# A gating layer's first projection as seven products instead of eight, and where GpSimd issues the sums of its weights

## The chip, the cores and the metric

The kernel runs on one core of a Trainium2 chip. The metric is the time of one execution in microseconds (us) on the device: 1015.75 us as the median of three runs of the kernel before (1014.75 to 1017.11). A run counts once; lower is better. Engines are called TensorE (PE in the rows), VectorE (DVE), ScalarE (ACT), GpSimd (POOL) and SyncE (SP). SP and POOL issue most of the transfers.

## The reference, cut to what matters

Four sublayers work on 512 tokens of 1024 channels, each followed by a residual sum and a layer norm. The one that the change rewrites is the second mixer:

```python
def chunked_spatial_gating(x, w_in, b_in, ln_g, ln_b, w_s, b_s, w_out, b_out):
    z = jax.nn.gelu(x @ w_in + b_in, approximate=False)
    u, v = jnp.split(z, 2, axis=-1)
    v = layer_norm(v, ln_g, ln_b)
    ...
    s = jnp.einsum("gts,bnsgc->bntgc", w_causal, v) + b_s.T[:, :, None]
    return (u * s) @ w_out + b_out

def reference(x, ...):
    for i in range(DEPTH):                       # DEPTH = 2
        y = conformer_conv_module(x, ...) if i == 0 else chunked_spatial_gating(x, ...)
        x = layer_norm(DEEPNORM_ALPHA * x + y, norm1_g[i], norm1_b[i])
        y = conv_ffn(x, ...)
        x = layer_norm(DEEPNORM_ALPHA * x + y, norm2_g[i], norm2_b[i])
    return x
```

`w_in` is 1024 x 2048. Its second half makes `v` (called GV below), its first half makes `u` (GU). All arithmetic is float32.

## The kernel before, in words

**Stages.** In order of time: the convolution's input projection with its 31 taps (to about 132 us), its output projection (to about 182), the first feed-forward (up to about 420, down to 531), gating (to about 670) and the second feed-forward (to the end).

**Weights.** All weights lie in DRAM as units of 128 x 1024 values (512 KB). A unit passes four steps: SP loads it into one of four `raw` slots (L532), ScalarE rounds it to its high part `wh` (`his`, L767), VectorE makes the low part `wl = raw - wh` (`los`, L1280), and TensorE uses it in three matmuls per tile: high x high, high x low, low x high. `w_used` counts the units that TensorE is done with, `w_lo` those whose low part is there. SP loads unit u only when the low part of unit u - 4 is made; ScalarE and VectorE write into the ring slot of unit u only when unit u - 4 of the ring is used. In the convolution some units have their low part made by an accumulating transfer that GpSimd issues (`lo`, L613).

**Strassen already in place.** The feed-forward's down projection takes seven products of half-size blocks instead of eight. Sums of its weight blocks are made in DRAM (`summed`): SP copies pieces of the units (`copies`, L538 to L540) and GpSimd issues accumulating transfers of 128 x 512 values on top (L702) and copies of that size (L704), one after the other as `w_used` advances (`summed_weights`).

**Gating before.** TensorE computes GV from eight units: the first four by token block (`down_by_block`), with the last transposes of the norm before in between, then four by channel (`down_by_k`); 192 matmuls of 512 columns. VectorE adds the bias row out of PSUM (L1943), ScalarE applies Gelu, VectorE takes statistics (L1948), and adds the scaled residual for later (`residual`, L1548, four instructions). After the last statistics VectorE aggregates them (L1958), GpSimd takes the roots of the four token blocks (`mixer_root`, L593 and L588), and VectorE normalizes block after block: L1962, L1966 (waits for the root), `los` of GU unit 4 + t, and the low part of v (L1970). Meanwhile TensorE computes the eight GU units of 24 matmuls each, waiting for each unit's low part; after the seventh it begins the spatial products (L2400), which need all four blocks of v.

**Orders are fixed by hand.** Each engine has one list of instructions, written out in the order of the code, and takes them strictly one after the other. A wait holds all that stands behind it on that engine, the issue of transfers on SP and GpSimd included. On GpSimd the convolution's part is, in this order: the adds of tap products for the last channel group, first token half (`add_last(0, ...)`), three adds for the second half, one `lo` transfer, four more adds, and the root of the first half (`mixer_root(0, 1, 0, HT)`), for which VectorE waits before it can centre the first token half (L1428).

The lines on which the prediction leans most, from the kernel before:

```python
        add_last(0, 1, LAST_GP[0])
        add_last(1, 1, 4)
        lo(BY_DMA[-1])
        add_last(1, 4, ROOT_AT)
        mixer_root(0, 1, 0, HT)
...
        for t in range(NT):
            mixer_root(ROOTS + 2 * NT + t, ROOTS + t + 1, t, 1)
```

## Time and profile before

| What | Value |
|---|---|
| median of 3 runs | 1015.75 us (1014.75 to 1017.11) |
| the profiled execution, its own time | 1015.58 us |
| its span (first to last instruction) | 1013.8 us |
| granted TensorE clock, share of full | 0.998 |
| TensorE matmuls, busy share of the span | 99% |
| VectorE | 86% |
| ScalarE | 60% |
| GpSimd | 23% |
| traffic of HBM over the span | 229 GB/s |

The profiled execution lies 0.17 us under the median, and 1.8 us of its time lie outside the span. The busy shares are averages over stages that differ; a matmul's record overlaps the next one's, so that the pace is read from distances between starts.

### The profile page before, as it was taken

Reading aid. Unit: us, or ns where it says so; the run is one execution under the profiler, and the core shown is the slowest. Engines: PE = TensorE matmul, PEld = TensorE weight load, DVE = VectorE, ACT = ScalarE, POOL = GpSimd, SP = SyncE. Lnnn points to the kernel's source line nnn. Section 1 sums busy time; section 2 is a strip of 40 time slices with the busy share of each in tenths; the row PEclk is TensorE's granted clock in tenths of the full one; section 3 lists DMA queues with packets and bytes.
Section 4 is the critical chain, followed back from the end, with each engine's and each line's share of the span. In section 5 each row is a group of like instructions: output and inputs, shape, how many; then the busy total and the mean of one; then the engine's idle time right before and its main releaser. Section 6 shows DMA issues by size and latency. Waiting matters only on the chain.

```text
span 1013.8 us, 15746 instructions
## 1 busy us (share of the span) xinstructions
PE 1003.6 (99%) x5379; PEld 861.1 (85%) x5379; DVE 867.6 (86%) x1228; ACT 604.5 (60%) x903; POOL 233.3 (23%) x289
## 2 busy tenths in 40 slices
PE   9999999999999999999999999999999999999997
PEld 7777788988899988888888888898988999888885
DVE  6999977897988988898894878779888888879888
ACT  7889865564565556666454343457555555566653
POOL 2998730023232121000010210002423212100001
PEclk9999999999999999999999999999999999999999
DMA  9766269369889676376555333825989966627652
GB/s 342 218 161 166 58 147 349 119 196 238 236 211 228 220 169 173 102 271 208 195 179 194 118 111 107 307 79 186 262 237 229 220 209 173 163 98 260 205 197 112
DMA packets 65590, 194.02 MB, mean 191 GB/s; under 512 B 7552, under 2 KB 8576, under 8 KB 65024
## 3 DMA queue, kind: packets, MB, share of 16 engines
q1 hardware_dynamic: 44144, 137.76, 39.1%
q0 software_dynamic: 19376, 48.24, 23.7%
q10 hardware_dynamic: 2016, 7.34, 2.1%
q8 instruction: 28, 0.46, 0.2%
q14 instruction: 26, 0.21, 0.1%
HBM read 178.11 MB, written 54.53 MB: 229 GB/s over the span
## 4 chain that ended last, share of the span: by engine, by line
PE 78%; DVE 5%; DMA 3%; issue 2%; ACT 1%; SPq 0%; DVEq 0%; POOL 0%; POOLq 0%; ACTq 0%
PE ps L2017 10%; PE ps L2018 10%; PE ps L2019 10%; PE ps L2306 6%; PE ps L2307 6%; PE ps L2308 6%; PE ps L2259 5%; PE ps L2260 5%; PE ps L2261 5%; PE ps L2027 4%; PE ps L2028 4%; PE ps L2029 4%; DMA raw<-d_weights 3%; PE ps L2186 1%; DVE ps L1618 1%
## 5 line engine op out<-in xcount | busy, mean ns | idle before, releaser
L2017 PE MATMUL ps<-xh,wh 128*128 128x512 f32 x528 | 208.5, 395 | 0.3 <-DVE wl L1280 0.3
L2018 PE MATMUL ps<-xl,wh 128*128 128x512 f32 x528 | 205.7, 390 | 0.0
L2019 PE MATMUL ps<-xh,wl 128*128 128x512 f32 x528 | 205.6, 389 | 0.0
L767 ACT ACTIVATE wh<-raw 128x1024 fp32r<-128x1024 f32 x114 | 119.9, 1057 | 80.4 <-PE ps L2308 49.5
L1280 DVE TENSOR_TENSOR wl<-raw,wh 128x1024 fp32r<-128x1024 f32 x101 | 123.2, 1224 | 32.9 <-ACT wh L767 32.5
L702 POOL DMA_DIRECT2D summed<-d_weights x88 | 75.2, 1115 | 198.0 <-PE ps L2019 96.4
L2017 PEld LDWEIGHTS ps<-xh,wh 128*128 128x128 f32 x528 | 99.2, 188 | 22.0 <-issue 1.2
L2019 PEld LDWEIGHTS ps<-xh,wl 128*128 128x128 f32 x528 | 99.1, 188 | 21.0
L2018 PEld LDWEIGHTS ps<-xl,wh 128*128 128x128 f32 x528 | 99.2, 188 | 20.7 <-issue 1.2
L2306 PE MATMUL ps<-wh,parts 128*128 128x512 f32 x264 | 102.9, 390 | 0.0
L2308 PE MATMUL ps<-wh,parts 128*128 128x512 f32 x264 | 102.7, 389 | 0.0
L2307 PE MATMUL ps<-wl,parts 128*128 128x512 f32 x264 | 102.7, 389 | 0.0
L1607 DVE TENSOR_TENSOR wl<-raw,wh 128x1024 fp32r<-128x1024 f32 x62 | 75.6, 1220 | 22.5 <-ACT wh L1014 22.5
L599 POOL TENSOR_SCALAR veps<-sqs 128x1 f32<-128x1 f32 x15 | 4.8, 323 | 385.2 <-ACT squares_down L961 266.2
L1376 DVE SCALAR_TENSOR_TENSOR ps<-glu,par,ps 128x512 f32<-128x512 f32 x125 | 84.7, 752 | 0.6 <-PE ps L2103 0.4
L622 POOL TENSOR_TENSOR gsum<-gsum,prods 128x512 f32<-128x512 f32 x53 | 70.2, 1324 | 14.5 <-ACT prods L836 8.4
L1014 ACT ACTIVATE wh<-raw 128x1024 fp32r<-128x1024 f32 x62 | 65.6, 1058 | 8.2 <-DMA raw<-d_weights 8.2
L1618 DVE SCALAR_TENSOR_TENSOR ps<-vpad,par,ps 128x512 f32<-128x512 f32 x80 | 60.3, 753 | 8.0 <-ACT ps L1038 2.2
L1618 DVE SCALAR_TENSOR_TENSOR ps<-gpad,par,ps 128x512 f32<-128x512 f32 x80 | 60.2, 753 | 6.4 <-DVE ps L1618 2.1
L2306 PEld LDWEIGHTS ps<-wh,parts 128*128 128x128 f32 x264 | 49.5, 188 | 11.1 <-DVE wl L1280 0.8
L2308 PEld LDWEIGHTS ps<-wh,parts 128*128 128x128 f32 x264 | 49.5, 188 | 10.4
L2307 PEld LDWEIGHTS ps<-wl,parts 128*128 128x128 f32 x264 | 49.6, 188 | 10.2
(266 smaller groups left out, 2543.9 us busy)
## 6 DMA issues: line engine op xcount, KB each, us to landing
raw<-d_weights SPq DMA_DIRECT2D x156, 512.0 KB, 4.9
raw<-summed SPq DMA_DIRECT2D x56, 512.0 KB, 4.1
summed<-d_weights POOLq DMA_DIRECT2D x88, 256.0 KB, 9.5
summed<-d_weights SPq DMA_DIRECT2D x66, 256.0 KB, 5.2
summed<-summed POOLq DMA_DIRECT2D x46, 256.0 KB, 4.8
res<-brow POOLq DMA_DIRECT2D x12, 512.0 KB, 10.7
wl<-raw POOLq DMA_DIRECT2D x4, 1024.0 KB, 6.9
wl<-raw POOLq DMA_DIRECT2D x5, 512.0 KB, 6.3
```

The costliest lines, as they stand in the source:

```text
L702: eng.dma_start(out, of, accum_op=ALU.add).then_inc(w_sum[i % AHEAD], 16)
L767: eng.activation(split_at(u)[0], raw[:, u % RAW, :], ACT.Copy).then_inc(w_hi, 1)
L1280: eng.tensor_tensor(l, raw[:, u % RAW, :], h.bitcast(f32), ALU.subtract).then_inc(w_lo, 1)
L1376: eng.scalar_tensor_tensor(out=ps[:, bank, :], in0=glu[:, j % 2, k:k + SEQ], scalar=par[:, c:c + 1], in1=ps[:, bank, :], op0=ALU.mult, op1 ...
L1607: eng.tensor_tensor(wl[:, slot, :], raw[:, part, :], wh[:, slot, :].bitcast(f32), ALU.subtract).then_inc(w_lo, 1)
L1618: eng.scalar_tensor_tensor(out=accs[v], in0=buf[:, off:off + SEQ], scalar=par[:, bass.ds(cw, 1)], in1=accs[v], op0=ALU.mult, op1=ALU.add). ...
L2017: eng.matmul(ps[:, bank, cols], a, xh[:, k, cols], start=(k == 0), stop=False)
L2018: eng.matmul(ps[:, bank, cols], a, xl[:, k, cols], start=False, stop=False)
L2019: mm = eng.matmul(ps[:, bank, cols], b, xh[:, k, cols], start=False, stop=(k == KD - 1))
L2306: eng.matmul(ps[:, bank + t, :], s_h, w_h[:, cols], start=first, stop=False)
L2307: eng.matmul(ps[:, bank + t, :], s_h, w_l[:, cols], start=False, stop=False)
L2308: mm = eng.matmul(ps[:, bank + t, :], s_l, w_h[:, cols], start=False, stop=last)
```

## The change

GV is computed by Strassen's scheme in Winograd's form: seven products of 256 tokens x 512 channels x 512 columns, 168 matmuls instead of 192. For that

- the weights of GV come as four units as before in another layout, two units of a fourth-product sum, four units with the sums for the fifth and sixth product, and four with those for the third and seventh: six units more than before, ten of them from a new DRAM tensor `gsum`. The first GU unit stands between the products as `U_GU0`;
- the sums in `gsum` are made by twelve SP copies of 128 x 512, issued behind the loads of the convolution's first four output units (`gv_copies`), by two accumulating transfers of 512 x 512 that GpSimd issues in the convolution, between the adds of the two token halves, and by ten more transfers that it issues behind the feed-forward's sums (`up_sums(0)`);
- sums of token blocks are made, rounded and split by VectorE and ScalarE (`gn5`, `gs2`, `gs4`, `gv7`), after copies of three blocks (`a11f`, `a12f`, `a22f`) by ScalarE;
- VectorE puts the products together in `vtm` (`gv_rd` counts);
- the residual's bias row of gating is added by four accumulating transfers that GpSimd issues, each behind a wait for one more used unit, and the scaling moves into the later sum (`half_sum`); the four VectorE instructions of `residual` are gone;
- some rows of parameters are loaded elsewhere in ScalarE's list.

The core of the diff (`...` where it is cut):

```diff
@@ build_trunk, SyncE
+        def gv_copies(i):
+            w1, w2 = weights_d[raw_gv + i], weights_d[raw_gv + GQ + i]
+            eng.dma_start(gsum_d[2 + i, :, 0:HALF], w1[:, 0:HALF]).then_inc(gv_copied, 16)
+            eng.dma_start(gsum_d[2 + GQ + i, :, HALF:UNIT], w2[:, 0:HALF]).then_inc(gv_copied, 16)
+            eng.dma_start(gsum_d[2 + GQ + i, :, 0:HALF], w2[:, HALF:UNIT]).then_inc(gv_copied, 16)
...
+            if u == U_GV + GQ:
+                eng.wait_ge(gv_sum, 16 * (4 + 2 * GQ))
             load(u % RAW, u)
+            if 0 <= u - U_CONV_OUT < GQ:
+                gv_copies(u - U_CONV_OUT)
@@ GpSimd, convolution
         add_last(0, 1, LAST_GP[0])
+        eng.wait_ge(gv_copied, 16 * 3 * GQ)
+        eng.dma_start(fifth[:, :, first], w2[:, :, first], accum_op=ALU.add).then_inc(gv_sum, 16)
+        eng.dma_start(third[:, :, second], w2[:, :, second], accum_op=ALU.add).then_inc(gv_sum, 16)
         add_last(1, 1, 4)
@@ GpSimd, behind the feed-forward's sums
         up_sums(0)
+        eng.wait_ge(gv_sum, 16 * 2)
+        eng.dma_start(fifth[:, :, second], fifth[:, :, first]).then_inc(gv_sum, 16)
+        eng.wait_ge(gv_sum, 16 * 3)
+        eng.dma_start(fifth[:, :, second], w2[:, :, second], accum_op=ALU.add).then_inc(gv_sum, 16)
...
@@ GpSimd, gating
         eng.affine_select(out=wsraw[:, :, :], ...
+        eng.wait_ge(br3_ok, 1)
+        eng.wait_ge(x_ok, 2 * NT)
+        eng.wait_ge(xt, 2 * 2 * NT)
+        for t in range(NT):
+            eng.wait_ge(w_used, U_GU + 1 + t)
+            eng.dma_start(res[:, t, :], brow[:, :], accum_op=ALU.add).then_inc(res3_add, 16)
         for t in range(NT):
             mixer_root(ROOTS + 2 * NT + t, ROOTS + t + 1, t, 1)
@@ VectorE, gating (the four residual instructions gone, among others these new)
-                residual(2)
+            eng.tensor_tensor(gn5[:, :, cols], ps[:, B0[1] + 2 * t, :].rearrange("p (k n) -> p k n", k=4), a22f[:, :, cols],
+                              ALU.subtract).then_inc(ga_sum, 1)
+            eng.tensor_tensor(gs2[:, :, cols], gn5[:, :, cols], a11f[:, :, cols], ALU.subtract).then_inc(ga_sum, 1)
...
+        eng.wait_ge(w_used, U_GU + 1)
+        for t in halves:
+            eng.wait_ge(gv_rd, G_C12 - 1 + t)
+            eng.tensor_tensor(vtm[:, 2 + t, c2], ps[:, 4 + t, :], vtm[:, 2 + t, c2], ALU.subtract).then_inc(gv_rd, 1)
@@ TensorE, gating
-        down_by_block(U_GV, 4, 4, xh, xl, 0, KD, last_block, lambda t: wait_x(1, t))
-        down_by_k(U_GV + 4, 4, 0, xh, xl, 0, KD)
+        def gv(u, c, bank, tokens, i, t):
...
+        for t in range(NT // 2):
+            wait_x(1, t)
+            for i in range(GQ):
+                if t == 0:
+                    eng.wait_ge(*lo_of(U_GV + i))
+                mm = gv(U_GV + i, 0, 4, g11, i, t)
...
+        eng.wait_ge(*lo_of(U_GU0))
+        eng.wait_ge(gv_rd, G_C11)
+        up(split_at(U_GU0), GU_BANK[0]).then_inc(w_used, 1)
...
+        for i in range(GQ):
+            gv_third(i)
+            if i == 0:
+                eng.wait_ge(gv_rd, G_MP4)
+            if i < GQ - 2:
+                gv_seventh(i)
+        gv_seventh(GQ - 2)
+        gv_seventh(GQ - 1)
...
-        for j in range(KD):
+        for j in range(1, KD):
             eng.wait_ge(*lo_of(U_GU + j))
```

How the lists of instructions move, at three places. First GpSimd in the convolution, from the adds of the first token half of the last channel group to the first root. Before (L631 are the adds, L613 the `lo` transfer, L593 and L588 the root):

```order
L622 TENSOR_TENSOR gsum<-gsum,prods 128x512 [waits gp_add,gp_prod] x5
L631 TENSOR_TENSOR gsum<-gsum,prods 128x256 [waits gp_add,gp_prod] x11
L613 DMA wl<-raw 128x1024 [waits w_neg]
L631 TENSOR_TENSOR gsum<-gsum,prods 128x256 [waits gp_add,gp_prod] x4
L593 TENSOR_SCALAR veps<-mv 128x2 [waits var_ok]
L588 TENSOR_TENSOR rstd<-veps,half_m 128x2 [waits eps_ok]
```

And now the same stretch of GpSimd, where L682 are the adds, L724 and L725 the new transfers and L644 and L639 the root:

```order
L673 TENSOR_TENSOR gsum<-gsum,prods 128x512 [waits gp_add,gp_prod] x5
L682 TENSOR_TENSOR gsum<-gsum,prods 128x256 [waits gp_add,gp_prod] x8
L724 DMA gsum<-d_weights 512x512 [waits gv_copied]
L725 DMA gsum<-d_weights 512x512
L682 TENSOR_TENSOR gsum<-gsum,prods 128x256 [waits gp_add,gp_prod] x3
L664 DMA wl<-raw 128x1024 [waits w_neg]
L682 TENSOR_TENSOR gsum<-gsum,prods 128x256 [waits gp_add,gp_prod] x4
L644 TENSOR_SCALAR veps<-mv 128x2 [waits var_ok]
L639 TENSOR_TENSOR rstd<-veps,half_m 128x2 [waits eps_ok]
```

Two transfers of 512 rows each have come to stand ahead of seven adds, one transfer and the root.

Second, GpSimd in gating, from the mask of the spatial weights to the roots of the four token blocks. Before (L743 is the mask, L593 and L588 the root of one block):

```order
L743 AFFINE_SELECT wsraw<-wsraw 128x1024 [waits gm_in]
L593 TENSOR_SCALAR veps<-mv 128x1 [waits var_ok]
L588 TENSOR_TENSOR rstd<-veps,half_m 128x1 [waits eps_ok]
L593 TENSOR_SCALAR veps<-mv 128x1 [waits var_ok]
L588 TENSOR_TENSOR rstd<-veps,half_m 128x1 [waits eps_ok]
```

And now on the same engine, with L815 as the transfers of the residual's row:

```order
L808 AFFINE_SELECT wsraw<-wsraw 128x1024 [waits gm_in]
L815 DMA res<-brow 128x1024 [waits xt,w_used,x_ok,br3_ok]
L815 DMA res<-brow 128x1024 [waits w_used] x3
L644 TENSOR_SCALAR veps<-mv 128x1 [waits var_ok]
L639 TENSOR_TENSOR rstd<-veps,half_m 128x1 [waits eps_ok]
```

Four transfers, each behind a wait for TensorE, have come to stand ahead of the roots.

Third, VectorE in gating behind those roots, as it is now (L2139 aggregates, L2143 and L2147 normalize block 0, L1395 is the low part of GU unit 4, L2151 that of v):

```order
L2139 BN_AGGR mv<-stats 128x2 [waits st_ok]
L2139 BN_AGGR mv<-stats 128x2 x3
L2143 SCALAR_TENSOR_TENSOR vtm<-vtm,mv,glg 128x1024 [waits var_ok,gm_in]
L2147 SCALAR_TENSOR_TENSOR vtm<-vtm,rstd,glb 128x1024 [waits rstd_ok,st_ok]
L1395 TENSOR_TENSOR wl<-raw,wh 128x1024 [waits w_hi,w_used]
L2151 TENSOR_TENSOR vl<-vtm,vh 128x1024 [waits v_hi]
```

This stretch stands as it stood before the change; only the line numbers differ.

## Rows read from the trace of the kernel before

**Rows 1.** The page: span; busy us (share of the span) xinstructions of each engine.

```profile
span 1013.8 us, 15746 instructions
PE 1003.6 (99%) x5379; PEld 861.1 (85%) x5379; DVE 867.6 (86%) x1228; ACT 604.5 (60%) x903; POOL 233.3 (23%) x289
```

**Rows 2.** Waits of TensorE, 400 to 1000 us: who for whom, us, times, longest.

```profile
PE ps L2351 <- DVE wl L1280: 0.2, 1, 0.2
```

**Rows 3.** Timeline of TensorE: start, us, line, xcount; start of GU and of spatial(0).

```profile
570.64 0.39 PE L2017 MATMUL ps<-xh,wh 128*128 128x512 f32 x1
...
608.72 0.28 PE L2400 MATMUL ps<-wsp,vh 128*128 128x256 f32 x1
```

**Rows 4.** Two stretches: length; PE, PEld, DVE, ACT, POOL busy; clock, DMA.

```profile
105.00:130.00 25.00, 24.89 (x149) 19.90 (x147) 24.59 (x47) 20.02 (x40) 19.61 (x23) 1.00 0.30 71
...
524.00:571.00 47.00, 47.00 (x220) 38.95 (x219) 31.17 (x38) 16.21 (x22) 4.16 (x5) 1.00 0.56 188
```

**Rows 5.** Timeline of GpSimd: residual row by transfers; the first root in gating.

```profile
284.66 3.59 POOL L687 DMA_DIRECT2D res<-brow  x4 [1.84 <-PE ps L2261]
...
577.86 0.24 POOL L593 TENSOR_SCALAR veps<-mv 128x1 f32<-128x1 f32 x1 [16.62 <-DVE mv L1958]
```

**Rows 6.** Timeline of VectorE in gating: residual, low parts, GV, behind the roots.

```profile
560.19 5.53 DVE L1548 SCALAR_TENSOR_TENSOR res<-res,brow 128x1024 f32<-128x1024 f32 x4
565.64 2.35 DVE L1280 TENSOR_TENSOR wl<-raw,wh 128x1024 fp32r<-128x1024 f32 x2
570.84 1.29 DVE L1943 TENSOR_TENSOR vtm<-ps,gvrow 128x512 f32<-128x512 f32 x2 [2.85 <-PE ps L2029]
...
579.70 1.29 DVE L1966 SCALAR_TENSOR_TENSOR vtm<-vtm,rstd,glb 128x1024 f32<-128x1024 f32 x1 [0.53 <-POOL rstd L588]
580.90 1.22 DVE L1280 TENSOR_TENSOR wl<-raw,wh 128x1024 fp32r<-128x1024 f32 x1
...
586.91 1.22 DVE L1280 TENSOR_TENSOR wl<-raw,wh 128x1024 fp32r<-128x1024 f32 x1
...
597.86 1.23 DVE L1970 TENSOR_TENSOR vl<-vtm,vh 128x1024 fp32r<-128x1024 f32 x1
```

**Rows 7.** Timeline of GpSimd, end of the convolution.

```profile
113.27 9.76 POOL L631 TENSOR_TENSOR gsum<-gsum,prods 128x256 f32<-128x256 f32 x11
123.46 0.87 POOL L613 DMA_DIRECT2D wl<-raw  x1 [0.43 <-ACT wl L769]
...
127.84 0.26 POOL L593 TENSOR_SCALAR veps<-mv 128x2 f32<-128x2 f32 x1
128.18 0.73 POOL L588 TENSOR_TENSOR rstd<-veps,half_m 128x2 f32<-128x2 f32 x1
```

**Rows 8.** Timeline, VectorE and TensorE, at the first centred block.

```profile
129.02 1.12 DVE L1428 TENSOR_SCALAR ctm<-ctm,mv,rstd 128x128 f32<-128x128 f32 x4
...
129.70 0.28 PE L2131 MATMUL ps<-gluh,diagl 128*128 128x256 f32 x1
129.82 0.38 PE L2170 MATMUL ps<-ident,ctm 128*128 128x128 f32 x2
```

**Rows 9.** Timeline of GpSimd: accumulating and plain transfers of 128 x 512.

```profile
228.12 1.65 POOL L702 DMA_DIRECT2D summed<-d_weights  x2 [3.47 <-PE ps L2261]
...
266.47 1.56 POOL L704 DMA_DIRECT2D summed<-summed  x3 [2.00 <-DMA summed<-d_weights]
```

**Rows 10.** L613, low parts by transfer: waits for it (us, times); time to landing.

```profile
  PEld ps L2017: 0.3, 1
...
DMA to landing us min/median/max: 4.4/6.8/8.6
```

**Rows 11.** Timeline of SP: loads in the convolution.

```profile
96.91 0.80 SPq L532 DMA_DIRECT2D raw<-d_weights  x2
```

**Rows 12.** SP's copies (L539), issue in ns and time to landing.

```profile
L539 SPq DMA_DIRECT2D summed<-d_weights x22: 587/598/1389, 152.3 to 702.2; - x22
...
DMA to landing us min/median/max: 3.9/5.2/10.5
```

More of the change, by code:

```diff
@@ L679, in _ @@
             eng.dma_start(res[:, t, :], brow[:, :], accum_op=ALU.add).then_inc(res0_ok, 16)
-        first, second = slice(0, HALF), slice(HALF, UNIT)
         issued = [0] * AHEAD
@@ L1150, in ffn_down @@
                     rows()
+                if layer == 0 and i == 2 * KQ + 5:
+                    eng.wait_ge(q_add, 6)
+                    row(gvrow[:, :], R_GVB, gv_in)
                 if i == KQ:
@@ L1542, in norm @@
                 block_lo(n, NT - 1)
-        def residual(n):
-            eng.wait_ge(bo_in, 16 * n)
-            for t in range(NT):
-                eng.scalar_tensor_tensor(out=res[:, t, :], in0=res[:, t, :], scalar=ALPHA, in1=brow[:, :],
-                                         op0=ALU.mult, op1=ALU.add).then_inc(res_ok, 1)
         def low_row(layer, q):
@@ new lines, in _ @@
+        los([U_G56 + 2])
+        eng.tensor_tensor(both_rows[:, :], gvrow[:, c1], gvrow[:, c2], ALU.add).then_inc(rows_ok, 1)
+        los([U_G56 + 3])
+        for t in halves:
+            token_lo(gs4l, gs4, gs4h, t, 4 + 2 * t + 1)
+            token_lo(gv7l, gv7, gv7h, t, 4 + 2 * t + 2)
+        los([U_G37])
+        eng.wait_ge(w_used, U_GU0)
+        eng.wait_ge(rows_ok, 1)
+        for t in halves:
+            eng.tensor_tensor(vtm[:, 2 + t, c2], vtm[:, 2 + t, c1], both_rows[:, :], ALU.subtract).then_inc(n_ok, 1)
@@ new lines, in _ @@
+        eng.wait_ge(gv_rd, G_M)
+        for t in range(NT // 2):
+            wait_x(1, 2 + t)
+            for i in range(GQ):
+                u = U_GV + GQ + i // 2
+                if t == 0 and i % 2 == 0:
+                    eng.wait_ge(*lo_of(u))
+                mm = gv(u, i % 2, 4, g22, i, t)
+                if t == 1 and i % 2:
+                    mm.then_inc(w_used, 1)
+        eng.wait_ge(*lo_of(U_GU0))
+        eng.wait_ge(gv_rd, G_C11)
+        up(split_at(U_GU0), GU_BANK[0]).then_inc(w_used, 1)
@@ new lines, in _, with gv_third @@
+        for i, t in ((0, 0), (1, 0), (0, 1), (1, 1), (2, 0), (2, 1), (3, 0), (3, 1)):
+            u = U_G56 + i
+            eng.wait_ge(ga_lo, 2 * t + 2)
+            if t == 0:
+                eng.wait_ge(*lo_of(u))
+            gv(u, 0, 0, gn5p, i, t)
+            mm = gv(u, 1, 2, gs2p, i, t)
+            if t == 1:
+                mm.then_inc(w_used, 1)
+        def gv_third(i):
+            eng.wait_ge(*lo_of(U_G37 + i))
+            for t in range(NT // 2):
+                mm = gv(U_G37 + i, 0, 6, gs4p, i, t)
+            if i == GQ - 1:
+                mm.then_inc(gv_pe, 1)
```

285 lines of the change are left out of this document (218 added, 67 removed).

## Prediction

> **What bounds the kernel now.** I read the page first: TensorE is busy for 99% of a span of 1013.8 us, VectorE for 86%, GpSimd for 23% [rows 1]. The waits of TensorE say how to take this: from 400 to 1000 us, which holds all of gating, it waits 0.2 us in all [rows 2]. So a matmul that is gone is time gained as long as no one else becomes late, and a new wait of TensorE is paid in full. The timeline gives the pace: from the start of GU to the start of spatial(0) lie seven units of 24 matmuls, 168 in 608.72 − 570.64 = 38.08 us, which is 0.2267 us a matmul or 5.44 us a unit [rows 3]. Then I looked for places where another engine stands just ahead of TensorE. In the convolution's last 25 us VectorE is busy for 24.59 and GpSimd for 19.61 [rows 4]; in GV's stretch VectorE has 31.17 of 47 us and GpSimd 4.16 [rows 4]. The sum is made against the profiled execution's 1015.58 us (1013.8 and 1.78 outside the span); the median of the runs is 0.17 us higher, which I let go.
>
> **1. The product itself: −5.44.** 192 matmuls become 168, all of the same shape: 24 x 0.2267 = 5.44 us. GU's first unit only changes its place.
>
> **2. GpSimd's four residual transfers in gating: +5.67.** Call E the end of GV's products, the first GU unit among them; that is 570.64 + 5.44 = 576.1 in terms of before's GV and GU0, but what counts are distances from E. The new L815 transfers wait for `w_used`, the first for E, the second to fourth for the ends of GU units 1, 2 and 3. Behind them on GpSimd stand the four roots; behind the first root on VectorE stand block 0's scaling (L2147) and then the low part of GU unit 4, which TensorE needs right after unit 3. This is a closed chain: TensorE finishes unit 3, and only then does work begin that unit 4 needs.
> Its length: wake GpSimd 0.11 (the gap between the root's end, 128.18 + 0.73, and VectorE's start at 129.02 [rows 7, 8]); issue of the fourth transfer 0.90 (3.59 / 4 [rows 5]); root to VectorE's start 579.70 − 577.86 = 1.84 [rows 5, 6]; scaling 580.90 − 579.70 = 1.20 and low part 1.22 [rows 6]; wake TensorE 0.11. The sum is 5.38. The convolution's root took 128.18 + 0.73 − 127.84 = 1.07, and 0.11 to wake VectorE [rows 7]: with it 4.7. I take 5.0. Before, this low part was ready at 582.12 and wanted at 570.64 + 4 x 5.44 = 592.4, so there were 10 us to spare, and the change uses all of them.
> From there VectorE needs 586.91 − 580.90 = 6.01 us to the next low part, where TensorE needs 5.44: +0.57. Spatial(0) stands behind unit 6 and waits for the last `vl`, which ends 597.86 + 1.23 − 580.90 = 18.19 after the first low part's start; TensorE is there 1.33 + 3 x 5.44 + 0.57 = 18.23 after it [rows 6]: +0.1 at most, for the wake. The residual's transfers themselves are wanted only by the later sums and cost nothing more.
>
> **3. VectorE in GV's stretch: +0.5.** It loses the four `residual` instructions, 5.53 us, and gets six more low parts at 2.35 / 2 = 1.18, which is 7.1, and by my count of the lists some 29 more instructions over 128 x 512 at 1.29 / 2 = 0.65, which is 18.7 [rows 6]. 31.17 − 5.53 + 7.1 + 18.7 = 51.4 of 47 us [rows 4]: VectorE is full, and part of its work runs over E. There the units' low parts 1 to 3 have already been made or have 5 us each, so that the surplus is mostly hidden, by the very wait of step 2 too. Inside GV the product sums stand one bank ahead of TensorE. Bounds: 0, and 1.8, which is one low part and one 512-column step late. I take 0.5.
>
> **4. Two transfers of 512 rows in the convolution: +4.07.** They stand behind 8 of the 11 adds, at 113.27 + 8 x 0.887 = 120.4, and ahead of three adds, the `lo` transfer, four adds and the root [rows 7]. VectorE starts L1428 0.11 us after the root, and TensorE takes the centred block at 129.82 with its last other matmul started at 129.70 [rows 8]: there is about 0.1 to spare. GpSimd's only idle time on the way is 0.43 ahead of L613 [rows 7]. So with x as the cost of one issue the path loses 2x − 0.53.
> No row shows an issue of 512 rows. From below, x is no less than that of an accumulating transfer of 128 rows, 1.65 / 2 = 0.82 [rows 9]; from above it is four times that, 3.3. A part of the 0.82 can't grow with the rows: L613 moves rows of 1024 elements for 0.87 [rows 7], so size is not what counts, and an accumulating issue costs 0.82 against 1.56 / 3 = 0.52 for a plain one [rows 9], as if it had more entries to write for the same rows. If the difference of 0.30 is what 128 rows of source add, and the rest behaves in part likewise, four times the rows come to 2.0 to 2.6. I take 2.3: 4.6 − 0.53 = 4.07. Bounds +1.1 and +6.1.
> The Trainium skill (DMA: Bandwidth & Descriptors, section "Anatomy of one DMA — SWDGE (gpsimd) path") speaks against me: it calls the generation of descriptors "small, variable", and one "can emit a lot of descriptors before the incremental cost shows up". By that the two issues would cost the lower bound. Another page (Perfetto Trace Analysis, section "DMA Instruction — SWDGE (GPSIMD)") says that the instruction's record ends when the last descriptor is generated, which leaves room for a duration that grows with the rows; no run here shows either yet.
>
> **5. SP's twelve copies in the convolution: +0.2.** They stand behind four loads, the last two at 96.91 [rows 11]. An issue takes 0.60 on SP's queue, a landing 5.2, at most 10.5 [rows 12], so that the last has landed by about 111 and GpSimd's new wait for `gv_copied` at 120.4 is met. But they share the DMA engines with the low parts made by transfer, which take 6.8 to land, at most 8.6, and for which TensorE waited 0.3 once [rows 10]. Bounds: 0, and 8.6 − 6.8 = 1.8. I take 0.2.
>
> **6. At no cost.** The ten transfers behind the feed-forward's sums: ten issues at 0.52 to 0.82, and four landings one after the other of up to 10.5 us, some 50 us on an engine that is idle for three quarters of the time [rows 1]; the units that come of it are loaded for GV, and the next root of GpSimd is wanted well over 100 us later. ScalarE's copies and rounding: 16.21 of 47 us are taken, so that some 25 more of about 0.6 fit [rows 4].
>
> **Sum.** −5.44 + 5.67 + 0.5 + 4.07 + 0.2 = +5.0, which gives 1020.6 us. With all low bounds −5.44 + 5.27 + 0 + 1.1 + 0 = +0.9 (1016.5), with all high ones −5.44 + 6.05 + 1.8 + 6.1 + 1.8 = +10.3 (1025.9).
>
> **The rivals.**
> A, an issue that hardly depends on its rows: x = 0.82, so that the convolution loses 1.1 and the whole is −5.44 + 5.67 + 0.5 + 1.1 + 0.2 = +2.0: 1017.6. For it: 0.87 for a transfer of twice the row length. Against: accumulating costs 1.6 times plain for the same rows.
> B, VectorE becomes the bound of GV's stretch: by step 3 it has 51.4 us of work, TensorE 47. If the product sums can't be put off, TensorE loses the whole surplus, 4.4 instead of 0.5, with x = 2.3: 1024.5. For it: the idle time of VectorE before GV's last read was 2.85 [rows 6], which is all that is left. Against: low parts of GU may slip.
> C, faster: TensorE does not wait at GU unit 4. This needs `w_used` to be met 5 us ahead of unit 3's last matmul, or VectorE to have the low part of unit 4 before the scaling; then −5.44 + 0.5 + 4.07 + 0.2 = −0.7 with x = 2.3, and −3.6 with x = 0.82: 1011.9. It decides only if less than 1.5 us of step 2's wait is left. Against it stand both lists, in which nothing can pass.
>
> **How the numbers follow.** Forecast 0.48, A 0.30, B 0.15, C 0.07. The likeliest gives 1020.6, with 1019.0 to 1023.0 as its own range. To hold the time 8 times in 10 the range takes in A and nearly all of B: 1016.2 to 1024.2. A difference under 0.2% (2.0 us) can't be told from none; the border is 1017.8. Two thirds of A lie under it, and nearly nothing of the forecast: same 0.20, faster 0.05, slower 0.75.
>
> **What the profile after would show.** Step 1: 24 matmuls fewer. Step 2: among TensorE's waits one of about 5 us for VectorE's `wl` (L1395) at the GU projection, and GpSimd idle at L815 four times for TensorE. Step 3: VectorE busy for nearly all of GV's stretch; several waits of over 0.5 us of TensorE there speak for B. Step 4: the durations of L724 and L725, and idle time of TensorE before L2351 or its centred blocks near 130 us, twice their duration less 0.5. Step 5: a wait for `wl<-raw` near 100 us. I am wrong if L724 takes under 1 us, or if the wait at GU unit 4 is under 3 us.

## The result, and the profile after

The changed kernel takes 1027.11 us (median of four runs, 1026.24 to 1034.85) against 1015.61 us before, 11.5 us more. By the means of the runs it is 1.0128 times as long, 95% interval 1.0099 to 1.0157. I had forecast 1020.6 us in a range of 1016.2 to 1024.2. The direction was right; the size was not, and the range missed it.

The profiled execution took 1026.85 us. Its page, with the lines that answer to [rows 1]:

```profile
span 1025.1 us, 15810 instructions
PE 1001.5 (98%) x5355; PEld 858.5 (84%) x5355; DVE 885.5 (86%) x1259; ACT 618.5 (60%) x924; POOL 245.3 (24%) x305
```

The 24 matmuls are gone, but TensorE's busy time fell by 2.1 us only, where 5.4 would be expected. The waits of TensorE over the whole run (who for whom, us in total, times, longest) say why it has become longer:

```profile
PE ps L2198 <- DVE wl L1395: 5.0, 2, 4.7
PE ps L2351 <- DMA wl<-raw: 4.5, 1, 4.5
PE ps L2327 <- POOL ident L657: 1.6, 1, 1.6
PE ps L2351 <- DVE ctm L1543: 1.1, 1, 1.1
PE ps L2366 <- DVE res L1643: 1.0, 1, 1.0
...
PE ps L2573 <- DVE wl L1395: 0.3, 1, 0.3
```

The first is the wait at GU unit 4 that step 2 spoke of. The second is as large, and no step of mine had it: TensorE, in the convolution's output projection, waits for a low part that a transfer of GpSimd (L664) makes. The timeline of TensorE around it (start, us):

```profile
136.64 0.40 PE L2210 MATMUL ps<-wh,xl 128*128 128x512 f32 x1
141.51 0.44 PE L2351 MATMUL ps<-ident,ctm 128*128 128x128 f32 x2 [4.48 <-DMA wl<-raw]
...
142.43 0.63 PE L2210 MATMUL ps<-wh,xl 128*128 128x512 f32 x1
142.86 0.63 PE L2208 MATMUL ps<-wh,xh 128*128 128x512 f32 x1
...
145.67 0.40 PE L2210 MATMUL ps<-wh,xl 128*128 128x512 f32 x1
145.90 0.40 PE L2208 MATMUL ps<-wh,xh 128*128 128x512 f32 x1
```

Two matmuls of 512 columns start 0.43 us apart behind the wait and 0.23 apart from 145.67 on. The granted clock says the same (window, length, busy us of PE, PEld, DVE, ACT, POOL, granted clock, DMA share, GB/s):

```profile
142.00:145.00 3.00, 3.00 (x11) 2.38 (x10) 0.19 (x1) 0.97 (x2) 0.00 (x0) 0.51 0.84 281
```

So behind the long wait comes a stretch at TensorE's lower level (1.2 GHz, a granted clock of 0.5), which costs another 1.6 us here; matmuls count as busy in it, which is why the busy time fell so little. The same stands behind the wait at GU unit 4, with 0.50 from 600.5 to 602.5:

```profile
594.80 0.39 PE L2200 MATMUL ps<-xh,wl 128*128 128x512 f32 x1
599.88 0.80 PE L2198 MATMUL ps<-xh,wh 128*128 128x512 f32 x1 [4.70 <-DVE wl L1395]
600.48 0.63 PE L2199 MATMUL ps<-xl,wh 128*128 128x512 f32 x1
...
602.95 0.39 PE L2199 MATMUL ps<-xl,wh 128*128 128x512 f32 x1
```

GpSimd at the places that the prediction spoke of, first in the convolution (to set beside [rows 7]), then in gating:

```profile
120.40 1.04 POOL L724 DMA_DIRECT2D gsum<-d_weights  x1
121.08 1.39 POOL L725 DMA_DIRECT2D gsum<-d_weights  x1
121.73 3.28 POOL L682 TENSOR_TENSOR gsum<-gsum,prods 128x256 f32<-128x256 f32 x3
124.95 0.88 POOL L664 DMA_DIRECT2D wl<-raw  x1
...
129.67 0.73 POOL L639 TENSOR_TENSOR rstd<-veps,half_m 128x2 f32<-128x2 f32 x1
...
595.49 0.86 POOL L815 DMA_DIRECT2D res<-brow  x1 [4.58 <-PE ps L2200]
596.42 0.24 POOL L644 TENSOR_SCALAR veps<-mv 128x1 f32<-128x1 f32 x1
```

The two large transfers start 0.68 and 0.65 us ahead of what follows them, but that is not all that they take of GpSimd. The first add behind them is recorded for twice the time of an add in the kernel before (first the kernel after, then the kernel before):

```profile
121.73 1.50 POOL L682 TENSOR_TENSOR gsum<-gsum,prods 128x256 f32<-128x256 f32 x1
```

```profile
120.53 0.73 POOL L631 TENSOR_TENSOR gsum<-gsum,prods 128x256 f32<-128x256 f32 x1
```

From the first issue to the end of that add, less 0.74 for the add, are 121.73 + 1.50 − 120.40 − 0.74 = 2.09 us, so x is 1.04 us. Put into the prediction's 2x − 0.53 this gives 1.6, and the root ended 1.49 us later than in [rows 7]. What was dear is not in that timeline but in the landings, in this order L724, L725 and L664 (for L664 the largest of nine is the one issued at 124.95; the same transfer landed after 4.4 us before the change, the slowest of the nine after 8.6 [rows 10]):

```profile
DMA to landing us min/median/max: 11.2/11.2/11.2
...
DMA to landing us min/median/max: 17.9/17.9/17.9
...
DMA to landing us min/median/max: 6.9/7.6/16.5
```

What the DMA engines do meanwhile stands in the sums by queue. GpSimd's queue from 120 to 140 us (packets, MB, share of the time of 16 engines):

```profile
q0 software_dynamic: 1191, 2.60, 84.3%
```

In these 20 us it is, but for one packet, the only queue at work: 2.6 MB keep the engines busy for most of the stretch. In the kernel before all queues together took some 30% of it.

VectorE in the stretch of GV (window, length, busy us of PE, PEld, DVE, ACT, POOL), to set beside [rows 4]: 46.38 of 47 us, full as forecast.

```profile
532.00:579.00 47.00, 46.72 (x214) 38.00 (x213) 46.38 (x65) 28.55 (x41) 3.39 (x5) 1.00 0.66 222
```

Last, the end. What GpSimd's sequencer does behind its last instruction, a drain, first of the kernel after, then of the kernel before:

```profile
L2673 POOLq DRAIN  x1: 6648/6648/6648, 1018.2 to 1018.2; - x1
L2673 SPq COMPARE_BRANCH  x1: 38/38/38, 1022.4 to 1022.4; - x1
```

```profile
L2426 POOLq DRAIN  x1: 3749/3749/3749, 1009.3 to 1009.3; - x1
L2426 SPq COMPARE_BRANCH  x1: 38/38/38, 1013.4 to 1013.4; - x1
```

SP's branch stands behind its wait for the last output. Before, GpSimd's drain had ended by then (1009.3 + 3.7 = 1013.0); now it ends 2.4 us behind the branch (1018.2 + 6.6 = 1024.9). The span ends 0.4 us behind the branch before and 2.7 us now, 2.3 us more.

Setting the same matmul of both timelines side by side gives the account. The lag is the start in the kernel after less that in the kernel before:

| Where | before | after | lag | what came to it |
|---|---|---|---|---|
| first centred block | 129.82 | 131.17 | 1.35 | root later; 0.2 had come up by 100 us |
| the matmul behind the wait for `wl<-raw` | 135.37 | 141.51 | 6.14 | +4.8, the wait |
| clock back | 137.65 | 145.42 | 7.77 | +1.6, half clock |
| first norm's transposes | 169.00 | 177.43 | 8.44 | +0.7 |
| last ones ahead of GV | 530.86 | 537.79 | 6.93 | -1.5, of which 1.0 near 263 us, where the kernel before waits 0.8 us and this one doesn't |
| end of GV and GU unit 0 | 576.08 | 578.71 | 2.62 | -4.3 = -5.44 + 1.1 |
| GU unit 4 | 592.40 | 599.88 | 7.48 | +4.9, the wait |
| clock back | 593.99 | 602.95 | 8.96 | +1.5, half clock |
| last matmul | 1006.61 | 1015.63 | 9.02 | |
| end of span | 1013.8 | 1025.1 | 11.3 | +2.3, the drain |

### The profile page after: what moved, and what is told of

Read it like the earlier page. It is cut to its first block, busy times and chain, and to the rows that moved or that the text cites. A ratio compares the mean times of both kernels' runs of the same rounds, so it can differ in the third digit from the quotient of the medians.

```text
span 1025.1 us, 15810 instructions
## 1 busy us (share of the span) xinstructions
PE 1001.5 (98%) x5355; PEld 858.5 (84%) x5355; DVE 885.5 (86%) x1259; ACT 618.5 (60%) x924; POOL 245.3 (24%) x305
## 4 chain that ended last, share of the span: by engine, by line
PE 89%; DMA 3%; DVE 3%; issue 2%; ACT 2%; SPq 1%; POOL 0%; DVEq 0%; ACTq 0%; POOLq 0%
PE ps L2198 13%; PE ps L2199 13%; PE ps L2200 13%; PE ps L2440 6%; PE ps L2441 6%; PE ps L2439 6%; PE ps L2486 6%; PE ps L2488 6%; PE ps L2487 6%; PE ps L2208 2%; PE ps L2209 2%; PE ps L2210 2%; PE ps L2284 2%; DMA wl<-raw 2%; DMA raw<-d_weights 1%
## 5 line engine op out<-in xcount | busy, mean ns | idle before, releaser
L838 ACT ACTIVATE wh<-raw 128x1024 fp32r<-128x1024 f32 x120 | 125.8, 1057 | 80.5 <-PE ps L2488 46.5
L1395 DVE TENSOR_TENSOR wl<-raw,wh 128x1024 fp32r<-128x1024 f32 x107 | 130.1, 1222 | 20.7 <-ACT wh L838 20.7
L1717 DVE TENSOR_TENSOR wl<-raw,wh 128x1024 fp32r<-128x1024 f32 x62 | 75.6, 1220 | 19.3 <-ACT wh L1092 19.3
L1092 ACT ACTIVATE wh<-raw 128x1024 fp32r<-128x1024 f32 x62 | 65.6, 1057 | 8.9 <-DMA raw<-d_weights 8.9
```

The source lines that it names most:

```text
L838: eng.activation(split_at(u)[0], raw[:, u % RAW, :], ACT.Copy).then_inc(w_hi, 1)
L1395: eng.tensor_tensor(l, raw[:, u % RAW, :], h.bitcast(f32), ALU.subtract).then_inc(w_lo, 1)
L1717: eng.tensor_tensor(wl[:, slot, :], raw[:, part, :], wh[:, slot, :].bitcast(f32), ALU.subtract).then_inc(w_lo, 1)
```

## The experiments

My theory from this profile (Q): the two large transfers delay the last `lo` transfer, which stood behind them in GpSimd's queue; the wait at GU unit 4 is the closed chain of step 2; the two are independent. Ratios are to the kernel before on the same chip, with their intervals. A profile is of one run each and can lie some us beside the median of its kernel, so the lags that I read from it (as in the table above) place a cost and do not add up to the medians.

### Each cost by itself

**sums_late**: the two transfers behind `up_sums(0)`.

```diff
@@ GpSimd, convolution
-        eng.wait_ge(gv_copied, 16 * 3 * GQ)
-        eng.dma_start(fifth[:, :, first], w2[:, :, first], accum_op=ALU.add).then_inc(gv_sum, 16)
-        eng.dma_start(third[:, :, second], w2[:, :, second], accum_op=ALU.add).then_inc(gv_sum, 16)
@@
         up_sums(0)
+        (the same three lines)
```

> The changed kernel with the two accumulating transfers of 512 rows issued behind the feed-forward's sums instead of in the convolution. Theory Q: the last low part made by transfer (L664, needed by TensorE at 137 us) stands behind these two in GpSimd's queue and landed after 16.5 us instead of 6.9; this costs the wait of 4.5 us, 1.6 us at TensorE's half clock behind it, and the issues 1.35 us. Then 1027.1 - 7.5 = about 1019.7, and no wait of TensorE near 137 us. Rival S: SP's twelve copies and loads crowd the DMA engines, the two transfers cost only their issue: about 1025.8, and the wait for wl<-raw stays.

Measured: 1024.06 us, 1.0083 (1.0067 to 1.0098). The wait near 137 us and its half clock are gone, and at 168.62 TensorE was 0.4 us ahead of the kernel before; but three new waits for `wl` came at 437 to 460 us, 1.5 us in all and 2.1 us of lag from 263 to 460 us, while ScalarE waits for loads of SP and the ten later transfers, which now wait 24 us for the landings of these two, are in flight. That profile's run took 1021.04, 3.0 under the median. So the convolution's share is right and the new place is not free; the size of the second is not sure.

**res_late**: the four residual transfers (with their waits) behind the roots of gating instead of ahead of them.

```diff
-        for t in range(NT):
-            eng.wait_ge(w_used, U_GU + 1 + t)
-            eng.dma_start(res[:, t, :], brow[:, :], accum_op=ALU.add).then_inc(res3_add, 16)
         for t in range(NT):
             mixer_root(ROOTS + 2 * NT + t, ROOTS + t + 1, t, 1)
+        (the same three lines)
```

> The changed kernel with the four residual transfers of gating moved behind the four roots. Theory: the closed chain at GU unit 4 goes, with 4.7 us of waiting and some 1.4 us at half clock behind it: 1027.1 - 6.2 = about 1020.9. Rival: the four transfers then start together when unit 4 or 5 runs and make loads late, or VectorE has no slack of its own there, and the gain is under 3 us: 1024 or more.

Measured: 1021.94 us, 1.0065 (1.0047 to 1.0082): 5.2 us less. From the end of GV to the last matmul the lag stayed at 4.0 us, where it had grown by 6.4. The chain of step 2 is shown, with its size. The expected gain was 6.2 us; in this profile 0.9 of lag had come up by 100 us (1.1 us against 0.2), ahead of all that the edit touches.

**both_late**: both moves.

> Both moves at once. If the two costs are independent: 1027.1 - 7.5 - 6.2 = about 1013.4, which is 2.2 us faster than the kernel before: the saved 5.44 us less 1.1 lost within GV and the longer landing of the last output write (4.4 us after its issue instead of 2.1 in the one profile each). If that landing is chance, about 1011. If the costs overlap, over 1016.

Measured: 1016.65 us, 1.0003 (0.9992 to 1.0013). In its profile (a run at 1019.67) the saving is eaten near 455 us:

```profile
PE ps L2486 <- DVE wl L1395: 3.6, 2, 3.1
```

ScalarE waited there for `raw<-summed`, a load of SP, while GpSimd's late sums were in flight. The new place brings this cost, 5.9 us of lag in this run; as the run is 3.0 us over the median, the usual cost is probably less, and that it explains the whole miss of the expected 1013.4 is not shown.

### Queue or shared engines

**sums_after_lo**: the two transfers right behind the last `lo`, still ahead of four adds and the root.

```diff
         lo(BY_DMA[-1])
+        (the wait and the two transfers)
         add_last(1, 4, ROOT_AT)
```

> The changed kernel with the two accumulating transfers issued right behind the last low part made by transfer, still ahead of four adds and the root. Theory Q (order in GpSimd's queue): the wait at 137 us goes with the half clock behind it, the issue's 1.3 us ahead of the root stay: 1027.1 - 6.1 = about 1021.0. Rival S (shared DMA engines, whatever the order): the wait stays mostly, 1025 or more.

Measured: 1025.13 us, 1.0085 (1.0068 to 1.0102). The wait for `wl<-raw` is gone, as Q says (L664 lands after 10.3 us at most), yet the time fell by 2.0 us only, where Q had 6.1: the wait for the root was 2.0 us, the wait for `res` ahead of the first norm 1.7, and new waits for `wl` near 458 us took 1.7 of lag. The two now landed after 15.9 and 23.3 us. Someone else paid.

**mid_both**: the two transfers behind the four residual transfers at the convolution's end, with res_late.

```diff
         for t in range(NT):
             eng.dma_start(res[:, t, :], brow[:, :], accum_op=ALU.add).then_inc(res0_ok, 16)
+        (the wait and the two transfers)
```

> The residual transfers of gating behind the roots, and the two accumulating transfers of 512 rows right behind the four residual transfers at the convolution's end (about 165 us) instead of in the convolution or behind the feed-forward's sums. Behind the feed-forward's sums they pushed the ten later transfers to 441 us and made loads late (TensorE waited 3.6 us near 455 us, and ran at half clock behind it). Expected: that goes, 1016.7 - 4.8 = about 1012. If the loads near 165 us suffer instead: 1016 or more.

Measured: 1032.50 us, 1.0154 (1.0139 to 1.0169), the slowest of all. TensorE's wait, and the landing of the second large transfer:

```profile
PE ps L2366 <- DVE res L1643: 15.5, 1, 15.5
```

```profile
DMA to landing us min/median/max: 34.1/34.1/34.1
```

The chain of waits leads over VectorE and ScalarE to a load on SP's queue:

```profile
158.35 18.90 DMA raw<-d_weights
```

The residual transfers ahead of the two landed in time (5.9 to 12.1 us). So it is not order in one queue alone: this load, in SP's queue, took 18.9 us. The four loads that SP issued from 158 to 178 us landed after 19.4 us (median), the five of the same stretch of the kernel before (156 to 176) after 9.5. In those 20 us the packets of GpSimd's queue took 61.6% of the engines' time for 1.85 MB and SP's 41.9% for 2.56 MB, where SP's had 95.4% and 6.81 MB before. The Trainium skill (DMA: Bandwidth & Descriptors, section "Queues, rings and completion order") says that each DMA engine takes packets in turn from the queues that have work for it; the shares fit that, and no run here shows the turns themselves. Theory Q was too narrow. What I then held (C): the two transfers take the shared DMA engines from whoever loads at that time.

**no_accum**: the changed kernel with both as plain copies, so that the sums lack this addend.

```diff
-        eng.dma_start(fifth[:, :, first], w2[:, :, first], accum_op=ALU.add).then_inc(gv_sum, 16)
+        eng.dma_start(fifth[:, :, first], w2[:, :, first]).then_inc(gv_sum, 16)
(and the second alike)
```

> The changed kernel with its two 512-row transfers in the convolution as plain copies (the sums come out without this addend). If the read of the target is what makes them hold the queue, the last low part behind them lands after about 11 us instead of 16.5, TensorE's wait for it falls from 4.5 us to under 1, and the time to about 1022. If a place in the queue is all that counts: 1027.

Measured: 1021.92 us, 1.0060 (1.0045 to 1.0075). They land after 8.0 and 9.8 us instead of 11.2 and 17.9, L664 after 9.9 at most, and TensorE's wait is gone. GpSimd's queue from 120 to 140 us, now for the same bytes:

```profile
q0 software_dynamic: 688, 2.62, 47.2%
```

That is 47.2% of the engines' time instead of 84.3%. The accumulation is what makes the two long and the engines full.

**one_early**: only the first of the two in the convolution, the second behind `up_sums(0)`.

> The changed kernel with the second of the two 512-row transfers behind the feed-forward's sums, the first in its place in the convolution. Half the dose: the last low part behind it lands after about 11.5 us instead of 16.5, which is just in time, so that the 4.5 us wait and the 1.6 us at half clock go and 0.7 of the issue: 1027.1 - 6.8 = about 1020.3, and up to 4 us more where the late transfer makes the feed-forward's loads late.

Measured: 1022.22 us, 1.0062 (1.0045 to 1.0078). L664 lands after 10.5 us at most, and no wait for it: half the dose fits, the whole doesn't. About 2 us of lag came back between 437 and 460 us, where the second transfer now goes.

**split**: eight transfers of 128 rows instead of two of 512, in the same place.

```diff
-        eng.dma_start(fifth[:, :, first], w2[:, :, first], accum_op=ALU.add).then_inc(gv_sum, 16)
+        for i in range(GQ):
+            eng.dma_start(fifth[i, :, first], w2[i, :, first], accum_op=ALU.add).then_inc(gv_sum, 16)
(and the second alike; the later waits count six more)
```

> The changed kernel with its two accumulating transfers of 512 rows in the convolution issued as eight of 128 rows. If the issue costs by the instruction (0.67 us each for 512 rows, 0.82 for 128 rows in other places): GpSimd loses 8 x 0.82 - 1.3 = 5.2 us more ahead of the root, and the last low part is as much later: about 1032. If it costs by the row: 1027. Drain of GpSimd at the end: by number of transfers 6.65 + 6 x 0.18 = 7.7 us, by rows 6.65 us.

Measured: 1029.57 us, 1.0132 (1.0116 to 1.0147). GpSimd's eight records start 0.53 us apart from 121.71 on, but they grow longer one by one, from 0.84 to 2.96 us, and the add behind them is recorded for 3.18 us:

```profile
125.98 3.18 POOL L682 TENSOR_TENSOR gsum<-gsum,prods 128x256 f32<-128x256 f32 x1
```

Less 0.74 for the add, the eight took 125.98 + 3.18 − 121.71 − 0.74 = 6.71 us, 0.84 each, against 1.04 for one of 512 rows. So four times the rows cost a quarter more. The wait for `ctm` rose from 1.1 to 5.7 us, by 4.6, which is 6.71 − 2.09. No wait for `wl<-raw` came: L664 was issued 5.9 us later and landed after 11.2 us at most, and TensorE was later too. The Trainium skill (DMA: Bandwidth & Descriptors, section "Anatomy of one DMA — SWDGE (gpsimd) path") has "a lot of descriptors before the incremental cost shows up", which the prediction quoted; these two prices agree with it.

### A place where nobody loads

**gap_both**: res_late, and the two transfers at 187 us, ahead of `up_sums(0)`.

```diff
         for t in range(NT):
             norm_root(ROOTS + t, t + 1, t)
+        (the wait and the two transfers)
         up_sums(0)
```

> Residual transfers of gating behind the roots; the two accumulating transfers of 512 rows at about 186 us, behind the roots of the first norm and ahead of the feed-forward's sums. In the kernel before the DMA engines are busy for 0.51 of the time from 180 to 190 us and 0.01 from 190 to 200. Theory C (the two take shared DMA engines from whoever loads at the time, wherever they stand in the queue): here nobody is late, and 1016.7 - 4.8 = about 1012. Rival: two such transfers cost some 5 to 15 us of lateness in any place, 1017 or more.

Measured: 1015.07 us over 12 runs, 0.9996 (0.9982 to 1.0010). The two land after 14.0 and 20.9 us, as late as elsewhere, and no wait of TensorE over 1 us is new: it is the place that counts. Theory C holds for this place, but the time is 3 us over what was expected. The 4.8 us were read from a profile of both_late that ran 3.0 us over its own median, so that the typical run probably had less to win. In gap_both's profile the lag is 1.4 us ahead of GV (1.6 had come up by 100 us, which no run explains; in the other profiles it is 0 to 2.3 there), GV gives 4.5 us (the lag goes from +1.4 to -3.1), and 2.3 of it go at the end.

### The drain at the end

All changed kernels so far had a drain of 6.65 us. These eight runs ask for its cause.

**mid_merged** (mid_both with each group of four residual transfers as one), **no_ten** (gap_both without the ten later transfers; their units are loaded unsummed), **rows_128** (gap_both, no transfer over 128 rows) and **gap_few** (gap_both, merged to 155 transfers).

```diff
-        for t in range(NT):
-            eng.dma_start(res[:, t, :], brow[:, :], accum_op=ALU.add).then_inc(res0_ok, 16)
+        eng.dma_start(res[:, :, :], (brow, repeated for the blocks), accum_op=ALU.add).then_inc(res0_ok, 16)
```

> As mid_both, and each group of four residual transfers on GpSimd (four groups: the convolution's end, two feed-forwards, gating) is one transfer of the four blocks, same rows and bytes: 12 transfers fewer. GpSimd's drain at the program's end took 3.75 us before (155 transfers) and 6.65 us in every changed kernel so far (171). Theory N: it grows with the number of transfers, 0.18 us each: drain about 4.5 us, and 2 us less in all, about 1010. Rival R: it grows with the rows moved: drain stays 6.65 us, about 1012.

> As gap_both, without the ten later transfers that make the other sums (the units that need them are loaded from the plain weights, so that the output leaves those sums out). By theory their cost in the feed-forward is nothing, as the trace of the changed kernel shows no new wait of TensorE between 390 and 530 us. GpSimd's drain at the end tells what sets it: 177 transfers and 171 both took 6.65 us, 155 took 3.75; if it follows packets (some 1500 fewer of 22704) it falls by about 1.5 us; if it is a step that the first extra transfers bring, it stays. Time: that of gap_both, less what the drain gives.

> As gap_both, with each of the four transfers of 512 rows (two in the gap at 186 us, two behind the feed-forward's sums) as four of 128 rows: the same bytes, 183 transfers instead of 171, none over 128 rows. Theory L: GpSimd's drain of 6.65 us comes of the large transfers, then it falls to about 4 us, which takes 2.4 us off the end: gap_both's time less 2.4. Rival P: it comes of how much the queue carried in all (22,704 packets instead of 19,376), it stays at 6.6 us and the time is that of gap_both.

> As gap_both, with the four groups of four residual transfers as one transfer each and the eight 128-row transfers of the fourth-product sums as four of 256 rows: 155 transfers by GpSimd, as many as in the kernel before, with the same bytes. GpSimd's drain so far against its transfers: 155 and 156 gave 3.75 us, 159 6.29, 161 6.49, 171 to 183 6.65. If the number decides, with a step between 156 and 159, the drain is 3.75 us here and the time is gap_both's 1015.1 less 2.4, about 1012.7. If something in the gating part or the amount moved decides, the drain stays over 6 us and the time at about 1015.

**before_512**, **before_16**, **before_4** and **before_accum**: the kernel before with more transfers of GpSimd into spare memory.

```diff
         for t in range(NT):
             norm_root(ROOTS + t, t + 1, t)
+        for i in range(16):
+            eng.dma_start(spare_d[i, :, 0:HALF], weights_d[i, :, 0:HALF]).then_inc(spare_in, 16)
         up_sums(0)
```

> The kernel before with one more transfer of 512 rows, a plain copy from the weights into memory that nobody reads, issued by GpSimd at 186 us, when the DMA engines are idle. Theory L: its drain of 3.75 us at the end goes to over 6 us and the time up by about 2.3 us (1018). Rival P: drain up by under 0.5 us, time as before (1015.7).

> The kernel before with sixteen plain copies of 128 rows of weights into memory that nobody reads, issued by GpSimd at 186 us, 171 transfers in all. If the number of transfers sets the drain: 6.65 us, time up by about 2.3 us. If it is something in the changed parts: 3.75 us, time as before. The feed-forward's loads may be a little late from the sixteen, 0 to 1 us.

> The same with four such copies, 159 transfers. By number: drain 6.29 us as in the other kernel with 159. By something else: 3.75 us.

> The kernel before with sixteen transfers of 128 rows into memory that nobody reads, four plain and twelve accumulating, with waits for their landings between the groups, four plain and four accumulating at 186 us and eight behind the feed-forward's sums, where the changed kernels have theirs. If accumulating transfers between DRAM tensors, or waits for them, bring the long drain: over 6 us. If it is something else in the changed program: 3.75 us, as with sixteen plain copies.

| Kernel | transfers of GpSimd | drain, us | time, us | ratio (interval) |
|---|---|---|---|---|
| before | 155 | 3.75 | | |
| before_512 | 156, one plain of 512 rows more | 3.75 | 1015.44 | 0.9995 (0.9984 to 1.0007) |
| before_4 | 159, four plain more | 3.75 | 1016.89, one run | |
| before_16 | 171, sixteen plain more | 3.75 | 1016.22 | 0.9999 (0.9988 to 1.0009) |
| before_accum | 171, four plain, twelve accumulating more | 8.20 | 1021.20, one run (before: 1017.13, one run) | |
| mid_merged | 159 | 6.29 | 1030.54 | 1.0147 (1.0131 to 1.0162) |
| no_ten | 161 | 6.49 | 1013.56 | 0.9982 (0.9972 to 0.9991) |
| gap_few | 155 | 6.29 | 1020.96 | 1.0048 (1.0031 to 1.0066) |
| gap_both | 171 | 6.65 | 1015.07 | 0.9996 (0.9982 to 1.0010) |
| rows_128 | 183 | 6.65 | 1014.35 | 0.9981 (0.9971 to 0.9991) |
| gap_vector (below) | 167 | 6.49 | 1013.19 | 0.9978 (0.9969 to 0.9987) |

Neither number nor rows set it: sixteen plain copies leave it at 3.75 us, and 155 transfers in the changed kernel leave it at 6.29. Nor do the packets of GpSimd's queue: 20,656 with 3.75 us (before_16), 21,008 with 6.49 (no_ten), 21,424 with 8.20 (before_accum), 22,896 with 6.65 (rows_128). Twelve accumulating ones into a DRAM tensor, with waits for their landings, brought it to 8.20 in the kernel before. Its row:

```profile
L2440 POOLq DRAIN  x1: 8200/8200/8200, 1011.0 to 1011.0; - x1
```

It ends 4.0 us behind SP's branch (1015.2). So these do bring it, in a kernel that has nothing else of the change. By which rule it grows stays open: the kernel before itself has 88 accumulating transfers into DRAM (L702) and 3.75 us, no_ten has just two more, of 512 rows, and 6.49 us, and whether the accumulation or the waits between the groups count was not told apart. gap_few also showed that merging is no gain: its transfers made several waits for loads (its lag is 2.2 us at 263 us, 4.6 at 460 and 5.3 at 492), and it is slower than gap_both. rows_128 is gap_both's equal within the scatter, and by its interval just faster than the kernel before.

**gap_vector**: gap_both with gating's residual row added by VectorE, four instructions of 128 x 1024 where it has idle time.

```diff
-        for t in range(NT):
-            eng.wait_ge(w_used, U_GU + 1 + t)
-            eng.dma_start(res[:, t, :], brow[:, :], accum_op=ALU.add).then_inc(res3_add, 16)
@@ VectorE
+        def residual_row(t):
+            eng.tensor_tensor(res[:, t, :], res[:, t, :], brow[:, :], ALU.add).then_inc(res3_add, 1)
         los(range(U_GU + 8, U_GU + 10))
+        residual_row(0)
         gated(0)
         gated(1)
         los([U_GU + 10])
+        residual_row(1)
...
+        residual_row(2)
+        residual_row(3)
         los(range(U_GOUT + 7, U_UP1 + 2))
```

> As gap_both, with the four residual transfers of gating gone from GpSimd: VectorE adds the row to each block in four instructions of 128 x 1024, two beside the spatial products and two ahead of the later sums (the next row's load waits for them). If these four transfers bring GpSimd's long drain (so far 6.29 us where the residual transfers are merged, 6.49 to 6.65 where they aren't, 3.75 in the kernel before with 155 to 171 transfers): drain 3.75 us and about 1012.7. If not: drain 6.6 us, and the time is that of gap_both (1015.1) or up to 2 us more, for 4.8 us of work on a VectorE that has some 3 us of idle time in that stretch.

Measured: 1013.19 us over 11 runs, 0.9978 (0.9969 to 0.9987): the fastest of all, and faster than both kernels, than the one before by 0.2%. The drain is 6.49 us, so these four transfers aren't its cause. Its page:

```profile
span 1011.7 us, 15809 instructions
PE 998.8 (99%) x5355; PEld 857.0 (85%) x5355; DVE 889.1 (88%) x1263; ACT 617.9 (61%) x924; POOL 241.9 (24%) x301
```

TensorE's busy time is 4.8 us under that of [rows 1]: the 24 matmuls without the half clock. VectorE carried the four additions of 1.22 us each without making TensorE wait. That this move is what made it 1.9 us faster than gap_both is not shown: both profiles hold their lag from the end of GV to the last matmul, and the 1.1 us between them had come up ahead of gating, where the two kernels are the same. What is shown is that it costs nothing.

## Why the prediction was wrong

By its own steps, in us:

| Step | forecast | measured |
|---|---|---|
| 1, the products | -5.44 | -5.44, from 24 matmuls fewer at the same pace |
| 2, GU unit 4 and behind it | +5.67 | +4.9 and +1.5 at half clock |
| 3, VectorE in GV | +0.5 | +1.1, of which one wait gives 0.4 |
| 4, two transfers in the convolution | +4.07 | +1.35 by the issue, +4.8 and +1.6 by the landing behind them |
| 5, SP's copies | +0.2 | not told from the scatter of the first 100 us |
| no step: lag around the norm and the feed-forward | | +0.7 and -1.5 |
| no step: drain | | +2.3 |
| sum | +5.0 | +11.3 |

**Step 4 failed, in its term.** It priced the two transfers by the time for which GpSimd is held, 2x − 0.53, and by nothing else. The formula held (x = 1.04 gives 1.6, the root came 1.49 later, TensorE lost 1.35), but x was 1.04 and not 2.3, near the 0.82 of rival A. What the step left out is their data: 2 MB that are added to 2 MB more and written, in flight when the last low part by transfer and the residual rows want the same DMA engines. That transfer landed after 16.5 us instead of 4.4, and TensorE waited 4.5 us for it. The 8.6 us landing of [rows 10] stood in step 5, as a risk of SP's copies, and [rows 8] showed that the whole stretch has no slack; I had both rows and did not ask what lies behind the two transfers in flight. no_accum, one_early and sums_late show it from three sides, mid_both that the other queues pay too. Of the measured 7.7 only the 1.35 come by the mechanism of the forecast 4.07; that a term too high stood against one left out brought the forecast nearer by luck. The two signs of being wrong that I had named did not speak (L724's record is 1.04 us, the wait at GU unit 4 is 4.7): neither asked for a landing.

**Step 2 was right**: the chain, its place and its 4.7 us (5.0 taken, 4.7 the lower of its ends; the root took the convolution's time). The further 0.6 and 0.1 didn't show: from 602.95 on the lag stays. What it lacked is what a wait of this length drags behind it: TensorE's clock at its lower level for some 3 us, 1.5 us of lag. The same term was missing at the other wait. Together 3.1 us.

**Step 3 was right that VectorE is full**, at 46.38 of 47 us, and 0.6 short. That VectorE's fullness is what TensorE paid for is shown in part: the profile has one wait there, for a low part (L2573, 0.3 us; the step from matmul to matmul is 0.67 us instead of 0.23). The rest lies in single steps of 0.34 to 0.39 us where a product changes its operands, with no wait recorded, and stays open. Rival B, which would have cost 4.4 us, did not come.

**The drain** stood in no step. The page doesn't show it, since a drain isn't counted as busy, and TensorE's last matmul is no place to stop the sum.

gap_both takes back 12.0 us by changing only where six transfers stand, so most of what made the change slower is their place. Two costs stay in it that the change as built brings along: some 1 us within GV and the 2.3 us of the drain. With them the 5.4 us of gain come to 2.1; by the medians gap_both is 0.7 us faster than the kernel before and gap_vector 2.6.

## What to carry to other kernels

Price a DMA three times: its issue on the engine (for GpSimd read up to the end of the instruction behind it, since the distance between starts is too short), its bytes on the shared DMA engines while others' loads are in flight, and what it leaves to do at the end. For the second, look up the DMA share of the stretch and who waits for a landing there with no slack; a stretch with free capacity but an urgent transfer is a bad place, one without any load is a good one. A wait of TensorE of 4 to 5 us cost a third more than its length in both cases here, by the clock behind it.

## What the runs showed of the hardware

- An accumulating transfer between DRAM tensors of 512 rows x 2 KB held GpSimd for 1.04 us, one of 128 rows for 0.84 (split), a plain one of 512 rows for 0.69 (no_accum: 122.63 + 0.76 − 121.28 − 0.74, halved): the issue grows by far less than the rows. The starts of such records lie closer (0.67 and 0.53 us), and the instruction behind pays the rest: an add of 0.74 us was recorded for 1.50 and 3.18.
- Two accumulating transfers of 512 rows at once landed after 11.2 and 17.9 us where no other queue had work, the same as plain copies after 8.0 and 9.8, and after 24.1 and 34.1 beside SP's loads, of which one took 18.9 us. In 20 us with the same 2.6 MB the queue took 84.3% of the DMA engines' time with accumulation and 47.2% without.
- After waits of 4.5 and 4.7 us TensorE ran at 1.2 GHz (granted clock 0.51 and 0.50) for about 3.5 and 3 us, with 0.43 us from matmul to matmul of 512 columns, then 0.23; after those of 1.0 and 1.1 us the granted clock stayed at 1.00.
- GpSimd's drain at the end took 3.75 us, 6.3 to 6.65 us and 8.20 us, the same to 0.01 us in kernels alike; twelve more accumulating transfers into DRAM (or the waits between them) made it longer, sixteen plain ones didn't; 88 accumulating ones of the kernel before leave it at 3.75.
